# Hybrid encoder layer: the stick-breaking columns of the input projection move into the delta rule's turns, as 24 pieces per tile

## The reference

```python
mod = silu(c) @ w_ada + b_ada                       # shift, scale, gate
h = rms_norm(x, g_pre_mix) * (1 + sc_m) + sh_m
proj = h @ w_in                                     # 3592 columns
# columns 0..1535     q, k, v of the delta rule, before a causal convolution of width 4
# columns 1536..2047  z, the delta rule's gate
# columns 2048..2055  b, g (4 heads each): beta and decay
# columns 2056..3591  q, k, v of stick-breaking attention (8 heads of 64)
oa = rms_norm(gated_delta_rule(qa, ka, va, g, beta, s0)) * silu(za)
ob = rms_norm(stick_breaking(qb, k_all, v_all))
x = x + gate * rms_norm(concat(oa, ob) @ w_out)
x = x + gate * rms_norm(hier_moe(h2))               # 32 experts, top 2
# outputs: y, and k, v of stick-breaking, the delta state, the last convolution rows
```

## Time and profile before

| what | us |
|---|---|
| median of three runs | 3951.24 (3949.82 to 3962.46) |
| profiled execution, own time | 3963.74 |
| its span | 3962.0 |
| PE busy in the span | 3418.8 (86%) |
| modulation, from the start to | 152 |
| projection, from 152 to | 1137 |
| masks and turn 0 of delta, from 1137 to | 1203 |
| delta turns 1 to 16, from 1203 to | 1749 |

### The profile page before, as it was taken

How to read it: one execution, slowest core, us unless ns; L and a number is a source line. 1 busy time by engine, 2 the same in 40 slices (tenths; PEclk the granted TensorE clock), 3 DMA queues, 4 the chain that set the end, 5 groups by cost and what they waited for, 6 DMA issues and landing times. The chain is left out here.

```text
span 3962.0 us, 52087 instructions
## 1 busy us (share of the span) xinstructions
PE 3418.8 (86%) x20837; PEld 2044.4 (52%) x20838; DVE 1227.9 (31%) x2190; ACT 892.9 (23%) x1332; POOL 475.8 (12%) x465
## 2 busy tenths in 40 slices
PE   5799999999978888858999899919999999999960
PEld 1454444445447777757888745504444444444430
DVE  0122130302124555548888623320000001000026
ACT  0021111111111111117888622201110111111011
POOL 0000000000013444322211000030000000000014
PEclk8779899998977888879999999959999999999985
DMA  7411111110111222221003023336576458635348
GB/s 281 147 34 40 58 40 45 50 40 35 40 49 60 89 89 89 89 73 45 27 26 107 15 98 122 106 144 236 190 260 256 175 202 323 246 127 214 111 154 301
DMA packets 223534, 478.79 MB, mean 121 GB/s; under 512 B 20032, under 2 KB 62664, under 8 KB 222342
## 3 DMA queue, kind: packets, MB, share of 16 engines
q1 hardware_dynamic: 170106, 327.12, 23.7%
q10 hardware_dynamic: 40096, 105.45, 6.8%
q0 software_dynamic: 13168, 43.84, 3.2%
HBM read 364.55 MB, written 111.81 MB: 120 GB/s over the span
## 5 line engine op out<-in xcount | busy, mean ns | idle before, releaser
L556 PE MATMUL p_pm<-hT,w_in 128*128 128x512 f32 (+1 forms) x1600 | 627.5, 560 | 8.3 <-ACT hT L451 5.3
L556 PEld LDWEIGHTS p_pm<-hT,w_in 128*128 128x128 f32 x1600 | 314.6, 221 | 319.5 <-issue 316.0
L2206 PE MATMUL e_py<-e_wd,e_hT 128*128 128x512 f32 x800 | 355.3, 597 | 16.5 <-ACT e_hT L2229 16.5
L2193 PE MATMUL e_pg<-e_wg,e_xT 128*128 128x512 f32 x800 | 353.0, 594 | 0.9 <-DVE e_xT L2250 0.9
L2193 PE MATMUL e_pu<-e_wu,e_xT 128*128 128x512 f32 x800 | 351.5, 592 | 0.0
L1609 DVE TENSOR_TENSOR_SCAN a_sums<-a_keep,a_beta 128x1032 f32<-128x1032 f32 (+1 forms) x138 | 319.1, 2312 | 32.7 <-ACT a_beta L1557 27.0
L2193 PEld LDWEIGHTS e_pg<-e_wg,e_xT 128*128 128x128 f32 x800 | 152.6, 191 | 192.9 <-issue 192.9
L1776 PE MATMUL x_po_<-w_out,x_mT 128*128 128x512 f32 (+1 forms) x544 | 244.3, 603 | 7.7 <-ACT x_mT L1819 7.7
L2193 PEld LDWEIGHTS e_pu<-e_wu,e_xT 128*128 128x128 f32 x800 | 152.0, 190 | 191.3 <-issue 191.3
L2206 PEld LDWEIGHTS e_py<-e_wd,e_hT 128*128 128x128 f32 x800 | 147.9, 190 | 194.2 <-issue 194.2
L2264 DVE TENSOR_TENSOR e_h_<-e_sg,e_pu 128x512 f32<-128x512 f32 x50 | 34.4, 687 | 655.2 <-PE e_pu L2193 655.2
(11 more groups left out here) (326 smaller groups left out, 3904.4 us busy)
## 6 DMA issues: line engine op xcount, KB each, us to landing
e_wg<-in_w_gate SPq DMA_DIRECT2D x32, 2048.0 KB, 11.4
e_wu<-in_w_up SPq DMA_DIRECT2D x32, 2048.0 KB, 16.3
e_wd<-in_w_down SPq DMA_DIRECT2D x32, 2048.0 KB, 21.0
y_d<-e_y_ ACTq DMA_DIRECT2D x50, 512.0 KB, 8.9
w_ada<-in_w_ada SPq DMA_DIRECT2D x12, 2048.0 KB, 15.3
y_d<-d_zero SPq DMA_DIRECT2D x16, 1024.0 KB
w_in<-in_w_in ACTq DMA_DIRECT2D x8, 1796.0 KB, 8.9
conv_d<-conv_out ACTq DMA_DIRECT2D x48, 256.0 KB, 2.1
```

Of the source, the lines that this page charges most:

```text
L556: mm = nc.tensor.matmul(p_mm[j % BANKS][:, 0:n], w[:, k, col:col + P], hT[:, k, 0:n], start=(k == 0), stop=(k == KT - 1))
L2193: mm = nc.tensor.matmul(out[:], xT[:, k, :], w[:, buf, k, :], start=(k == 0), stop=(k == KT - 1))
L2206: mm = nc.tensor.matmul(p_y[c][:], hT[:, f, :], wd[:, buf, f, c * (D // 2):(c + 1) * (D // 2)], start=(f == 0), stop=(f == FT - 1))
```

## The change

Projection multiplies only the delta rule's columns (0 to 2055). Its order is new: slabs 0 and 1 first, then the sample tokens, then slabs 2 and 3. hT has two buffers, and the four tiles of the next slab are loaded, squared, normalised, turned and scaled between the 12 convolution groups of the running slab. z is multiplied in two halves of 260 columns, with b and g as the last 8 columns of the second. The sample tokens are multiplied with 32-column weights, four column blocks side by side. ACT's square root becomes a power on GpSimd. Each tile's hT is stored to DRAM (`hT_d`).

In delta, the sums of the decays are made once, for all tiles, before the first turn. SP loads the three weight blocks of stick-breaking (2 MB each) in turn 0 and one 512 KB tile of hT per turn. In turns 1 to 16 TensorE multiplies the tile's v, k and q in 24 pieces: 8 for v and 8 for k (one matmul of 512 columns each), 8 for q (four matmuls of 128 columns each). The pieces share one PSUM tile, `PB`; ScalarE copies v, k and q out of it, and k is turned at the end of the turn into `keysT`. SP stores v, k and q of a tile one turn after its own. The sample tokens' v, k, q are multiplied after the last turn. The products of the tail are in a new order (`kV` ahead of `aV`, the next turn's `kk` ahead of both), the masks stage moves ahead of modulation, and zeros for `y_d` go out from a quarter of the former row.

```diff
...
-                    act.dma_start(g.w_in[:, k, :], w_in[:, k, :]).then_inc(g.s_w_in, 16)
+                    act.dma_start(g.w_a[:, k, :], w_in[:, k, 0:g.OFF_QB]).then_inc(g.s_w_a, 16)
...
+    groups = []
+    for s in range(SLABS):
+        groups += [("conv", s, j) for j in range(CT)] + [("z", s, t, half) for t in range(TT) for half in range(2)]
+        if s == NEW_AFTER:
+            groups += [("new", i) for i in range(4)] + [("new_bg",)] + [("new_turned", i) for i in range(3)]
...
+        def coming(s, j, first):
+
+            t = (j - first) // 2
+            return (s + 1, t) if s + 1 < SLABS and (j - first) % 2 == 0 and 0 <= t < TT else None
...
+                def turn_rows(tile):
+                    q, n = place[tile], size(tile)
+                    pe.wait_ge(s_xn, q + 1)
+                    if q:
+                        pe.wait_ge(s_h, q)
+                        pe.wait_ge(s_h2, q)
+                    for k in range(KT):
+                        last = nc.tensor.transpose(p_x[:, k, 0:n], x[q % RING][0:n, k * P:(k + 1) * P], g.ident[0:n, 0:n])
+                    last.then_inc(s_xt, 1)
...
+                        for k in range(KT):
+                            for j in range(QUARTERS):
+                                col = (i * QUARTERS + j) * P
+                                mm = nc.tensor.matmul(out[j * NEW:(j + 1) * NEW, 0:P], hTn[:, k, :], w[:, k, col:col + P],
+                                                      start=(k == 0), stop=(k == KT - 1))
...
+                for s in range(SLABS):
+                    for j in range(CT):
+                        channels(s, j)
+                        if coming(s, j, 3):
+                            turn_rows(coming(s, j, 3))
                     for t in range(TT):
+                        gates(s, t)
...
+                for s in range(SLABS):
+                    for j in range(CT):
+                        convolve(s, j)
+                        if coming(s, j, 1):
+                            mean(coming(s, j, 1))
+                        if coming(s, j, 2):
+                            normalise(coming(s, j, 2))
+                        if coming(s, j, 5):
+                            scaled(coming(s, j, 5))
...
+        FIRST, PIECES, LATE = 1, {1: (2, 2), 2: (1, 2), 3: (1, 2), 4: (1, 2), 5: (2, 2), 6: (2, 1)}, (1, 2)
...
+                def store_b(tile):
+                    at = slice(tile * P, (tile + 1) * P)
+                    sp.wait_ge(act_p.sem, act_p(tile, "v"))
+                    sp.dma_start(g.outs["v_prompt"][at, :], g.values[:, tile, :]).then_inc(s_store["v"], 16)
+                    sp.wait_ge(act_p.sem, act_p(tile, "k"))
+                    sp.dma_start(g.outs["k_prompt"][at, :], k_rows[:]).then_inc(s_store["k"], 16)
...
+                        for u, col in enumerate((g.OFF_VB, g.OFF_QB + g.ROWS, g.OFF_QB)):
+                            sp.dma_start(w_b[u][:], w_in[:, :, col:col + g.ROWS]).then_inc(s_wb[u], 16)
                     done(sp, dve_c, turn - 1, "o_z")
                     sp.dma_start(zt[0:n].rearrange("p h d -> p (h d)"), g.z_d[at, :]).then_inc(s_z, 16)
+                    if turn >= 2:
+                        store_b(turn - 2)
...
+                def take_b(turn, part):
+                    tile = turn - 1
+                    done(act, pe_p, tile, part)
+                    if part != "kT" and part != "v" and tile:
+                        act.wait_ge(s_store[part], 16 * tile)
...
+                    def __call__(self, pieces):
+                        turn, tile = self.turn, self.turn - 1
+                        if turn == 0:
+                            return
+                        for piece in range(self.at, self.at + pieces):
+                            u, i = divmod(piece, KT)
...
+                            if i == 0:
+                                if turn == 1:
+                                    pe.wait_ge(s_wb[u], 16)
+                                done(pe, act_p, *((tile - 1, "kT") if u == 0 else (tile, PARTS[u - 1])))
+                            h = hb[turn % 2]
+                            if u < 2:
+                                mm = nc.tensor.matmul(PB[:].rearrange("p h d -> p (h d)"), h[:, i, :], w_b[u][:, i, :], start=(i == 0), stop=(i == KT - 1))
+                            else:
+                                c, ks = i // 2, range((i % 2) * KT // 2, (i % 2 + 1) * KT // 2)
+                                for k in ks:
+                                    mm = nc.tensor.matmul(PB[:, c, :], w_b[u][:, k, c * P:(c + 1) * P], h[:, k, :], start=(k == 0), stop=(k == KT - 1))
...
                 def body(turn, follows):
                     later, n, tile, at = shape(turn)
+                    fill = Filler(turn)
+                    fill(FIRST)
                     for l in range(1, LEVELS - 1):
-                        level(turn, l)
+                        level(turn, l, fill, *PIECES[l])
                         if follows and l in (2, 3, 4):
-                            (a_rows, a_sums, a_decay)[l - 2](turn + 1)
-                    join(turn)
+                            (a_rows, a_values, a_decay)[l - 2](turn + 1)
+                    join(turn, fill, *PIECES[LEVELS - 1])
...
+                    if follows:
+                        b_query_products(turn + 1)
+                    if later:
+                        keys_over(turn)
...
```

More of the change, by code:

```diff
@@ L336, in projection @@
[L336 to L339, removed]
+    BANKS = 6
+    RING = 3
+    ZA = (g.ROWS + 2 * DN_HEADS) // 2
+    NEW_AFTER = 1
+    QUARTERS = P // NEW
+    tiles = [(s, t) for s in range(NEW_AFTER + 2) for t in range(TT)] + ["new"] + [(s, t) for s in range(NEW_AFTER + 2, SLABS) for t in range(TT)]
@@ new lines, in projection @@
+    place = {tile: q for q, tile in enumerate(tiles)}
+    groups = []
[3 more added lines that the diff above has]
+            groups += [("new", i) for i in range(4)] + [("new_bg",)] + [("new_turned", i) for i in range(3)]
+    number = {group: k for k, group in enumerate(groups)}
+    s_w, s_small = g.s_w_a, g.sem("p_small")
+    s_x, s_sq, s_ms, s_r, s_xn = [g.sem(f"p_x{r}") for r in range(RING)], g.sem("p_sq"), g.sem("p_ms"), g.sem("p_r"), g.sem("p_xn")
@@ L363, in projection @@
[L363 to L389, removed]
+        bank = [g.psum(f"p_pm{b}", [P, 512], at=life) for b in range(BANKS)]
+        def size(tile):
+            return NEW if tile == "new" else P
+        def tokens(tile):
+            return slice(g.SEQ, g.TOK) if tile == "new" else slice(tile[0] * SLAB + tile[1] * P, tile[0] * SLAB + (tile[1] + 1) * P)
@@ L838, in _ @@
+                turns(sp, load_ct, body, end)
+                sp.wait_ge(s_zeros, (1 + FILL * g.TILES) * 16)
+                for part in ("v", "k", "q"):
+                    sp.wait_ge(s_store[part], 16 * g.TILES)
+                sp.wait_ge(s_new_out, 16 * (1 + 2 * P // NEW))
             @block.scalar
@@ L984, in b_products, with b_query_products @@
                     mm.then_inc(pe_b.sem, pe_b.did("L"))
-                def level(turn, l):
+                def b_query_products(turn):
+                    later, n, tile, at = shape(turn)
+                    done(pe, act_b, turn, "qdT")
+                    done(pe, dve_c, turn - 1, "state")
+                    for h in range(H):
+                        mm = nc.tensor.matmul(X[1][0:n, h, 0:n], knT[:, h, 0:n], qnT[:, h, 0:n], start=True, stop=True)
+                    mm.then_inc(pe_b.sem, pe_b.did("kq"))
@@ L987, in level, with keys_over @@
+                def keys_over(turn):
+                    tile = turn - 1
+                    done(pe, act_p, tile, "q")
+                    for c in range(H):
+                        tr = nc.tensor.transpose(PB[:, c, :], k_rows[:, c * P:(c + 1) * P], g.ident[:])
+                    tr.then_inc(pe_p.sem, pe_p.did("kT"))
+                def level(turn, l, fill, between, after):
                     later, n, tile, at = shape(turn)
@@ L1012, in level, with join @@
                         mm.then_inc(pe_b.sem, pe_b.did(f"TLT{l}{half}"))
-                def join(turn):
+                    fill(after)
+                def join(turn, fill, between, after):
                     later, n, tile, at = shape(turn)
```

811 lines of the change are left out of this document (440 added, 371 removed).

## The result

The median went from 3950.53 us (4 runs, 3949.09 to 3962.46) to 3717.01 us (4 runs, 3713.12 to 3718.07): a ratio of 0.940, 95% interval 0.938 to 0.942. The forecast was 3767, in a range of 3665 to 3865. The profiled execution took 3716.6 us (span 3714.6), where the sum gave 3780: 63 us less than forecast.

A forecast was written before the change was run, and what follows sets the result against it. Projection was bound by TensorE's matmuls near full clock, delta turns by a chain of short steps with holes. 3963.7 − 402 − 21 + 222 + 2 + 15 = 3780, less 12.5 for the median: 3767 us, range 3665 to 3865.

The forecast's parts named there:

- Projection's sum: Projection stage: terms 461 + 24 + 51 + 24 + 23 make 583 us instead of 985, giving 402 us back.
- The nine holes: Projection, slabs 0 to 2: TensorE waits for VectorE's scaling, 5.7 us each, 51 in all, plus 24 of lost clock.
- Rival 2: Projection: scaling is done by the time TensorE asks, so no stall; 75 us less, 3692; chance 0.12.
- The sample tokens: Projection: the sample tokens' 128 matmuls with 32-column weights take 20 us, plus 3 for waits.
- Preparation: Start of projection: loading, normalising, transposing and scaling the first slab's four tiles takes 24 us.
- Modulation: Modulation stage, waiting for DMA: pairs shorten from 26.4 to 21.1 us, giving 21 us back, bounds 12 and 25.
- A turn: Delta stage: one turn takes 48.0 us, bounds 43 and 52, against 34.15; 16 turns cost 222 us more.
- k's copy and L: Delta turn: TensorE stalls 1.5 us in level 5 for ScalarE's copy of k, and `L` waits 0.3 for VectorE's LT.
- Changing between small and full blocks: Delta turn: eight new pairs of changes between 64x64 blocks and the full array, 0.29 us each, cost 2.3 us.
- Rival 1: Delta turns: the pieces cover no waits, so a turn takes 57.85 us, total 3924; chance 0.08.
- Rival 3: Delta turns: the clock stays low, a turn takes 67.5 us, 534 more, total 4079, slower; chance 0.06.
- Delta's end: After the last delta turn: loading hT, multiplying the sample tokens, copies, transposes and stores cost net 15 us, 8 to 25.

The follow-up runs named there:

- The last experiment: Changed kernel with earlier scaling and earlier keys' transposes, plus first slab's tiles 0 and 1 scaled before the fourth is squared and normalised: 3628.64 us, ratio 0.918.
- three pieces: Changed kernel multiplying only the last of the eight pieces each of v, k and q per turn, 3 instead of 24: 3529.96 us, ratio 0.893.
- three lumps: Changed kernel with the same 24 pieces per turn in three groups of eight instead of ones and twos between levels: 3818.13 us, ratio 0.967.

## Why the prediction held, step by step

- **Projection's sum**: right in its large parts, 17 us too high. The groups and z cost what was worked out: the slab without holes is 112.7 with its tail, for 111.8 without transposes. The nine holes were found from the order of the three lists: 46 us in nine waits of 5.1 (5.7 forecast), and the earlier scaling shows both the cause and their clock. Together they cost 68 us of the 75 forecast. Rival 2 (no stall, −75) was a wrong description of this kernel; scaling one group earlier makes it true, for 69 us.
- **The sample tokens**, 20 + 3: the mis-sized term. They took 8.0 with what follows them: 0.028 for an instruction of 128 columns, where the prediction had 0.111 without overlap and 0.067 with that of the 64x64 blocks. The Trainium skill ("TensorE: Matmul & The Clock Gate", Part 3) gives 2.38 for three column tiles of 512 columns. Here four of 128 columns gain 3.0 by the order of the loops alone. The prediction's estimate of 12 us by that page was nearer than the 20 taken.
- **Preparation**, 24: took 32.7. The first transposes came 146.16 − 134.50 = 11.7 us into it, 9.6 being forecast. The rest, missed, was that both engines square and normalise all four tiles before they scale the first, and that the fourth tile's load needs a buffer that tile 0 must leave: one hole of 8.2 us. The last experiment shows it by their order alone.
- **Modulation**, −21: its pairs come every (100.66 − 21.34) / 4 = 19.8 us, 6.6 less than in the earlier trace rows, 26 in four pairs. It ends only 17.5 earlier since the masks now lie ahead of it. Why the period fell below the 21.1 worked out from the bytes wasn't tried.
- **A turn**, 48.0: took 46.2, the forecast without a loss of clock being 46.7. The step that took a value between 46.7 and 50.0, for a clock that is low in part, was wrong: PEclk is 1.00 and no low stretch is left. TensorE's part was a little larger (725.5 / 16 = 45.3 busy against 20.2 + 21.0 + 0.4 + 2.3 = 43.9) and the waits smaller: 0.77 at the border for 1.0, and next to nothing of the 1.5 + 0.3 for k's copy and L. With 24 pieces ScalarE's copy of k was released by the store of the tile before in 6 turns only, and TensorE waited for that copy once, 0.7 us; with three pieces it costs 2.5 us a turn. What the new order of the tail and the decay sums made ahead give by themselves was not tried. ScalarE's waits for that store in the changed kernel (us in total, times, longest):

```profile
ACT d_krows L960 <- DMA out_k_prompt<-d_krows: 22.7, 6, 12.5
```

- **Changing between small and full blocks**, 0.29 per pair: 16 instructions of 64x64 take 1456.86 − 1456.25 = 0.61, where 0.53 is 16 of the 0.033 that the earlier trace rows give; four instructions of pieces (two pieces) take 1.91 instead of 1.74. That is 0.25. The Trainium skill ("TensorEngine Tiling (Array Packing)", Tiling Modes) says that a change of tiling mode drains TensorE. The trace agrees, with these 0.25 us for a pair. The three lumps show that the cover is worth far more than the changes.
- **Rival 1** (the pieces cover nothing, 57.85 a turn) falls by the turn of 46.2; how much they cover is shown by the lumps (101 us) and by the three pieces (12.0 to 14.5 us for 18.4 of work and the changes).
- **Rival 3** (the clock stays low in delta) falls by the granted clock of 1.00. What speaks for its danger: in lumps the same work has 0.94.
- **Delta's end**, 15: 6.6. From `wT` of turn 16 to the first instruction after delta it is 1511.23 − 1488.42 = 22.8 us, and was 1755.03 − 1738.79 = 16.2. The 192 instructions with four column blocks took some 7 us (1.93 for 64 of them at full speed), not 13 to 21.

The sum was 63 us too high: 15 of it in the sample tokens, 24 in the turns, 10 in modulation and what lies between projection and the turns, 8 at the end, and the rest in small terms of both signs; among them preparation's 9 too few offset the holes' 7 too many. That the forecast of 3767 was off by only 50 is luck: it took 12.5 us off the sum because the profiled execution of before lay that far above its median, and that of the changed kernel lies 0.4 below.

## What to carry to other kernels

Where an engine waits in many short gaps, cut other work of it into pieces of the gaps' size and issue them there: that hides part of the work and can keep the clock up (here 24 pieces cost some 12 us a turn for 21 of work). The same work in three lumps lost 6.4 of those 9 us again, with the clock at 0.94. Once the profile shows no gaps, each further piece costs all of its time. And read the lists of the engines side by side at each buffer that is handed round: a consumer that stood one iteration too late cost 7.5 us each time here, and moving it up by one gave that back.

## What the runs showed of the hardware

- Instructions in four 32-column blocks that take turns overlap: 256 of them (128 f32 matmuls of 128 columns) take 7.20 us, 0.028 each, against 0.086 when 16 in a row (eight matmuls) stand in the same block.
- A stage of 739 us of f32 matmuls that mixes 64x64 blocks, 128-column and 512-column instructions kept a granted clock of 1.00, with 13 us of waits in all and none over 0.8 us; the same work in lumps, with 80 us of waits of up to 1.6 us, had 0.94.
